# A planner's clock that counts changes of the array's shape, and a ten-point plan of pace for the side work, in a two-block transformer kernel

## The reference

```
x = first_block(x, ...)     # per layer: mixer, layer norm, FFN of 4096, layer norm, gated embedding
x = second_block(x, c, ctx, ...)
# second_block:
for i in range(2):
    mod, mod_c = silu(c) @ w_mod[i] + b_mod[i], silu(c_ctx) @ w_mod[i] + b_mod[i]
    h  = rms_norm(x)  * (1 + sc1)  + sh1
    hc = rms_norm(xc) * (1 + sc1c) + sh1c
    y, yc = token_mixers(h, hc, ...)   # linear attention, neighbourhood and window attention;
                                       # x's three read keys, values and end states of the context
    x = x + g1 * y;  x = x + g2 * swiglu(...)
    if i == 0:
        xc = xc + g1c * yc;  xc = xc + g2c * swiglu(...)
return rms_norm(x, final_norm)
```

## Time and profile before

| | |
|---|---|
| median of 3 runs | 1847.15 us (1845.49 to 1847.87) |
| the profiled execution | 1849.54 us, its span 1848.2 us |
| mean granted TensorE clock | 0.989 |
| TensorE, VectorE, ScalarE busy | 97%, 69%, 54% |
| moved from memory | 331.36 MB, 180 GB/s over the span |

### The profile page before, as it was taken

How to read it: one execution, slowest core, us unless ns; L and a number is a source line. 1 busy time by engine, 2 the same in 40 slices (tenths; PEclk the granted TensorE clock), 3 DMA queues, 4 the chain that set the end, 5 groups by cost and what they waited for, 6 DMA issues and landing times. The chain is left out here.

```text
span 1848.2 us, 35695 instructions
## 1 busy us (share of the span) xinstructions
PE 1783.7 (97%) x14792; PEld 1662.9 (90%) x14792; DVE 1275.3 (69%) x2350; ACT 990.8 (54%) x1741; POOL 76.8 (4%) x81
## 2 busy tenths in 40 slices
PE   7999999999999999999899999999999999989997
PEld 6778899978989999999889987899999998679997
DVE  5566556658779855876676777766677777876665
ACT  4555545456556644654655655554455565644443
POOL 0000100020000200000100001000000000100000
PEclk9999999999999999999999999999999999999999
DMA  9797866686434565455455453445656543236663
GB/s 375 277 346 247 319 189 184 191 287 199 126 115 151 152 185 183 136 161 187 132 173 160 143 166 103 149 160 185 189 177 199 165 149 107 87 116 184 184 185 122
DMA packets 93857, 334.73 MB, mean 181 GB/s; under 512 B 10992, under 2 KB 12976, under 8 KB 93568
## 3 DMA queue, kind: packets, MB, share of 16 engines
q1 hardware_dynamic: 92016, 327.33, 55.4%
q0 software_dynamic: 1680, 5.11, 0.9%
HBM read 331.36 MB, written 1.05 MB: 180 GB/s over the span
## 5 line engine op out<-in xcount | busy, mean ns | idle before, releaser
L565 DVE TENSOR_TENSOR low<-ring,high 128x1024 fp32r<-128x1024 f32 x410 | 501.3, 1224 | 218.6 <-ACT high L557 209.6
L590 PE MATMUL bank<-XHx,high 128*128 128x256 f32 x2096 | 608.2, 290 | 20.9 <-DVE low L565 8.7
L591 PE MATMUL bank<-XLx,high 128*128 128x256 f32 x2096 | 592.0, 282 | 0.0
L592 PE MATMUL bank<-XHx,low 128*128 128x256 f32 x2096 | 590.9, 282 | 0.0
L557 ACT CAST high<-ring 128x1024 fp32r<-128x1024 f32 x410 | 428.4, 1045 | 272.4 <-PE bank L592 225.8
L590 PEld LDWEIGHTS bank<-XHx,high 128*128 128x128 f32 x2096 | 397.7, 190 | 39.3 <-issue 9.1
L591 PEld LDWEIGHTS bank<-XLx,high 128*128 128x128 f32 x2096 | 398.1, 190 | 1.6 <-issue 0.2
L592 PEld LDWEIGHTS bank<-XHx,low 128*128 128x128 f32 x2096 | 398.1, 190 | 0.0
L590 PE MATMUL bank<-XHc,high_side 128*128 128x256 f32 x608 | 180.9, 298 | 9.6 <-DVE low_side L565 7.4
L591 PE MATMUL bank<-XLc,high_side 128*128 128x256 f32 x608 | 172.0, 283 | 0.0
L592 PE MATMUL bank<-XHc,low_side 128*128 128x256 f32 x608 | 171.8, 283 | 0.0
(11 more groups left out here) (448 smaller groups left out, 3054.3 us busy)
## 6 DMA issues: line engine op xcount, KB each, us to landing
ring<-in_stream SPq DMA_DIRECT2D x410, 512.0 KB, 3.7
ring_side<-in_stream SPq DMA_DIRECT2D x110, 512.0 KB, 3.7
ring_mod<-in_stream SPq DMA_DIRECT2D x96, 512.0 KB, 7.8
x_nb<-in_rpb POOLq DMA_DIRECT2D x6, 256.0 KB, 3.5
x_late_NB<-in_rpb POOLq DMA_DIRECT2D x6, 256.0 KB, 3.2
Xx<-in_x SPq DMA_DIRECT2D x2, 512.0 KB, 5.5
Xc<-in_ctx SPq DMA_DIRECT2D x1, 1024.0 KB, 6.6
out<-y SPq DMA_DIRECT2D x8, 128.0 KB, 2.0
```

The costliest lines, as they stand in the source:

```text
L565: nc.vector.tensor_tensor(st.low[:, j % st.n_ring, :], st.ring[:, j % st.n_ring, :], st.high[:, j % st.n_split, :].bitcast(F32), ALU.subtr ...
L590: nc.tensor.matmul(out, wh, xh, start=(i == 0), stop=False)
L591: nc.tensor.matmul(out, wh, xl, start=False, stop=False)
L592: m = nc.tensor.matmul(out, wl, xh, start=False, stop=(c == ks[-1]))
```

## The change

Three things change. TensorE's lane remembers how many rows and columns of the array the last matmul used; `shape(rows, cols)`, called ahead of each matmul or group of them, adds 0.2 us to the clock when they differ. The costs of matmuls are new: `T_us` divides by 2370 and has no added 0.006, a product's passes cost `n / 2180` each, the 64-row and 64-column matmuls of the recurrence 0.03 us each, and the modulations lose 0.45 us per four tiles. And both plans of pace have new points. No instruction, buffer, semaphore or size is added, removed or changed; only the order in the engines' queues and the numbers that hang on it can differ.

```diff
+    def shape(self, rows, cols):
+        if (rows, cols) != self.rows_cols:
+            self.clock += SHAPE_US
+            self.rows_cols = rows, cols
...
 def T_us(n, passes=1):
-    return max(n * passes / 2270.0, 0.06) + 0.006
+    return max(n * passes / 2370.0, 0.06)
+
+
+def pass_us(n):
+    return n / 2180.0
+
+
+SHAPE_US, QUARTER_US = 0.2, 0.03
...
+            T.shape(P, P)
             nc.tensor.matmul(out, wh, xh, start=(i == 0), stop=False)
...
-                m.then_inc(*T.tick(k.s_products, 3 * T_us(n), key, *used))
+                m.then_inc(*T.tick(k.s_products, 3 * pass_us(n), key, *used))
...
+                T.shape(P, 32)
                 T.wait_ge(k.s_raw_mod[tile % RING_MOD], k.marks["mod raw", tile])
...
-                if c % MOD_BATCH == 0:
-                    T.spend(0.45)
...
+            T.shape(HD, P)
             for step in range(len(parts[0])):
...
                 us = T_us(SEQ - q0, 4 // len(one))
+                T.shape(P, P // len(one))
...
-                        m.then_inc(*T.tick(k.s_mixers, T_us(CH, 2), (tag(i), "inner scores", hh)))
+                        m.then_inc(*T.tick(k.s_mixers, QUARTER_US, (tag(i), "inner scores", hh)))
...
-MOD_PLAN = [(0, 0), (120, 16), (200, 48), (385, 72), (440, MOD_TILES)]
-SIDE_PLAN = [(480, 0), (840, 35), (1300, 94), (1530, 110)]
+MOD_PLAN = [(0, 0), (120, 16), (180, 56), (395, 72), (450, MOD_TILES)]
+SIDE_PLAN = [(480, 0), (600, 11), (725, 23), (845, 40), (960, 50), (990, 64), (1200, 80), (1295, 99), (1410, 100), (1535, 110)]
```

More of the change, by code:

```diff
@@ L633, in rows_product @@
             if c == DC - 1:
-                m.then_inc(*T.tick(k.s_products, 3 * T_us(n), keys[i], *mine))
+                m.then_inc(*T.tick(k.s_products, 3 * pass_us(n), keys[i], *mine))
             elif mine:
-                m.then_inc(*T.tick(st.s_used, 3 * T_us(n), *mine))
+                m.then_inc(*T.tick(st.s_used, 3 * pass_us(n), *mine))
             else:
-                T.spend(3 * T_us(n))
+                T.spend(3 * pass_us(n))
             yield None
@@ L1596, in tensor_hgrn @@
     k.bank_of[tag, "inner"] = b0
+    T.shape(P, CH)
     for i in range(2 * NQ):
@@ L1620, in tensor_hgrn @@
         r = slice(j * CH, (j + 1) * CH)
+        T.shape(CH, P)
         for h in range(2):
@@ L1833, in tensor_gla @@
                 k.bank_of[tag(i), "inner", hh] = yield from w.banks.take(T, (tag(i), "masked", hh))
+            T.shape(HD, CH)
             for c in range(CHUNKS):
@@ L1856, in tensor_gla @@
             s = slice(j * CH, (j + 1) * CH)
+            T.shape(CH, P)
             nc.tensor.matmul(k.bank[banks[j]][:, tile * P:(tile + 1) * P], keT[s, tile, :],
                              V_[s, tile, pair * P:(pair + 1) * P], start=True, stop=True).then_inc(
-                *T.tick(k.s_states, T_us(P, 4), (tag(i), "step", n)))
+                *T.tick(k.s_states, T_us(P, 3), (tag(i), "step", n)))
         yield None
@@ L1869, in tensor_gla @@
         halves = [slice(hh * HD, (hh + 1) * HD) for hh in range(2)]
+        T.shape(P, HD)
         for tile in range(NQ):
@@ L1884, in tensor_gla @@
                 state = S[:, n - 1, :]
+            T.shape(HD, HD)
             for hh, r in enumerate(halves):
@@ L1887, in tensor_gla @@
                                      one["q"][r, c * CH:(c + 1) * CH], start=False, stop=True, skip_group_check=True)
-                T.spend(T_us(CH, 2))
+                T.spend(QUARTER_US)
         m.then_inc(*T.tick(k.s_values, 0.0, (tag(i), "sums")))
```

7 lines of the change are left out of this document (4 added, 3 removed).

## The result

The changed kernel takes 1851.2 us (median of 9 executions, 1847.67 to 1856.45), the kernel before 1845.56 beside it (9 executions, 1843.93 to 1848.56). The ratio is 1.0022 with a 95% interval of 1.0012 to 1.0032, so it is slower, by a little. The forecast was 1839 us.

A forecast was written before the change was run, and what follows sets the result against it. TensorE, busy 97% of the span, was taken as the bound. Terms -7.6 + 1.5 - 2 = -8.1 from the profiled 1849.5 gave 1841.4; the median lies 2.4 lower, so 1839 us, range 1827 to 1854.

The forecast's parts named there:

- 845 to 1000: Stretch with two long TensorE waits for side tiles and low clock behind them: -7.6 us, bounds 0 and -15.2.
- Shape changes: Changes of array shape between matmuls, whole kernel: no step orders by them, 0 us, bounds -2 and +2.
- What the time can change by: Whole kernel: TensorE's work is constant; only idle time, lower-clock time and shape-change cost can move.
- What moves the order is mostly the table: Planner: the clock's two corrections nearly cancel, net about 2 to 10 us, so the plan's new points set the order.
- The side work follows the plan closely: Splits of side tiles: the plan sets them, on a clock some 20 to 30 us below the profile's time.
- Modulations: Modulation tiles, judged at 180 us: already ahead of the old plan, so cost 0, bounds -1 to +1.
- The small waits: Some 10 us of TensorE waits besides the two long ones: as many new as removed, 0, bounds -6 and +6.
- The surge: Plan's 14 side tiles in 30 us from 960: only 6 or 7 possible, so +1.5 us, bounds 0 and +10.
- The end of the side work: Last side product some 4 us earlier, leaving more x work to cover last-layer attention: -2 us, bounds -4 and +4.
- Slower by the surge: Rival: TensorE stands at late-landing side tiles, +7 to +10 us, 1854 to 1857 with long waits kept; chance 0.19.
- More changes of shape: Rival: side products between x's small recurrence matmuls after 990, +4 us, 1851; chance 0.07 with other losing reorderings.
- Nothing measurable: Rival: the two long waits only move with x's norms; 1843.5 to 1850.8, about 1847 us; chance 0.18.

The follow-up runs named there:

- before_again: The kernel before, unchanged, run and profiled a second time: ratio 1.0006 [0.9998, 1.0015] to the kernel before.
- clock_late: Changed kernel with both old plans, and old matmul costs and free shape changes once all 110 side tiles are used: 1.0089 [1.0070, 1.0107] to the kernel before.
- after_again: The changed kernel, unchanged, run and profiled again: ratio 1.0013 [1.0001, 1.0026] to the kernel before, median 1850.18 us.

## Why the prediction was wrong

The time lay inside the range of 1827 to 1854, but it moved the other way than was forecast. Two terms of the sum failed: *845 to 1000*, put at -7.6 us and worth -2.6, which new waits elsewhere took back, and *Shape changes*, put at 0, where the last stretch grew by 3.9.

*What the time can change by* was right. All traces have 14,792 matmuls, and the spans differ by idle time and by matmuls at the lower clock.

*"What moves the order is mostly the table"* was wrong, and it is the main error. I had summed the clock's corrections to a net of 2 to 10 us and taken that as small. The clock alone gave 1.0080 and 1.0092, the table alone 1.0006. 4 us of the plan's place are enough for 0.5 to 0.8%, so a net of 2 to 10 us is not small.

*"The side work follows the plan closely"* was wrong before 845: 31 splits and not 37. The distance of the planner's clock from the profile's time, 20 to 30 us, was also worked out too small: with 3 to 5.5 tiles missing or unused at 0.1 to 0.13 tiles per us the same rows give some 30 to 55 us. Between 725 and 845 there are 10 splits in both kernels. My guess from the stage times is that the contexts' attention, which must end first, holds the work there; no run tested it.

*Modulations, 0:* held. The old modulation plan gave 1.0009 [0.9999, 1.0019] beside 1.0013 [1.0001, 1.0026].

*845 to 1000, -7.6:* failed; it carried the forecast. The wait by VectorE's order fell from 5.4 to 3.4 us, the wait for the DMA stayed (4.4 and 4.5). Together 9.8 became 7.9, 1.9 less. The low clock behind them cost 5.4 us and now costs 0.30 of 5.6 and 0.50 of 6.0, 4.7. That makes 2.6 us and not 7.6. *The small waits, 0:* failed too. The other waits for side tiles grew, from 2.5 to 5.9 us and in the second traces from 3.6 to 5.1; the largest of them is one of 2.95 us at 1212, in both traces of the changed kernel, where before has 1.0 and 1.3. The wait of 1.9 us for `c_gla_end` is new as well. Up to V idle time didn't change.

*The surge, +1.5:* 5 splits in its 30 us for 3, where 6 or 7 were forecast, and no wait for `low_side` between 980 and 1120 in either trace, so the cost that was forecast isn't there. Without the point the ratio is 1.0043.

*The end of the side work, -2:* the sign was wrong in effect. c's last product did come 4 us earlier in the profiled execution, at 1556.6 for 1560.8, but before_again, with the old order, has it at 1556.4: that was no effect of the order. What came in that place is +3.9 us behind it.

*Shape changes, "no step orders by them", 0 with bounds -2 and +2:* this is where the loss is. The price moves TensorE's lane against VectorE's in the planner, and so it can shift the splits among the softmax steps. Taking it away behind the side work is worth 5.5 to 7.5 us of the last stretch over the two traces of either kernel, and 0.38% between the ratios. It is shown that in this order the price causes the block. By which tie in the planner it does so was not followed, and clock_late shows that the block can come without it.

*Rivals.* "Slower by the surge" is excluded: between 980 and 1120 TensorE waits for no side tile, and the kernel without the surge is no faster. "More changes of shape" names the time, 1851, but not the cause: the order of TensorE has not more changes than before (277 by the same count that gave 285). The Trainium skill (TensorEngine Tiling (Array Packing), Key Properties) says that a change of mode drains TensorE; the trace agrees with a cost of about 0.09 us, but what the price did to VectorE's queue outweighs it. "Nothing measurable" is nearest for the middle.

**What stays open.** Six neighbours of the changed kernel under the new clock (points 4 us earlier, 4 us later, no surge, the price at 0.1 and at 0, the old plans) are all slower than it, by 0.2 to 1.0% and each with waits of its own. A seventh, with only the old modulation plan, is not slower (1.0009). That fits points chosen for this very clock among many orders. Why the old clock is less touchy (1.0006 and 1.0021 for its two neighbours) isn't settled by two runs.

## What to carry to other kernels

Where a planner orders engines by an estimated clock and a table of times is set against that clock, the two are one thing: change one and the whole order is drawn anew, here for -0.3 to +1.2%, even where the correction is small, so time the neighbours too before you believe in a mechanism. Compare stretches that hold the same matmuls, not windows of equal time: it put a loss of 0.2% into one place, though executions of one order differ by as much. And a more faithful price is not a better one where the planner doesn't act on what it prices: free behind the side work and 0.2 us ahead of it gave 0.9973 and 0.9975, the best of all.

## What the runs showed of the hardware

The same order with the same wait can be followed by the lower clock or not. Around 1209 the changed kernel waits 2.95 us for a side tile in both its traces. In the first the clock stays at 1.00:

```profile
1209.40:1213.40 4.00, 1.17 (x9) 1.17 (x10) 4.00 (x9) 3.23 (x7) 0.00 (x0) 1.00 0.44 131
1213.40:1217.00 3.60, 3.60 (x33) 3.60 (x32) 3.60 (x8) 2.37 (x5) 0.00 (x0) 1.00 0.02 5
```

In after_again it falls to 0.50, 1.2 GHz:

```profile
1209.60:1213.70 4.10, 1.52 (x12) 1.52 (x13) 4.10 (x10) 3.40 (x7) 0.00 (x0) 1.00 0.44 132
1213.70:1217.10 3.40, 3.40 (x18) 3.40 (x17) 3.40 (x8) 1.37 (x4) 0.00 (x0) 0.50 0.00 0
```

Half of such a stretch is lost, 1.7 us. The kernel before has two of them (at 188.8 and 1199.1) which before_again, the same program, doesn't have; at 1.7 us each that is most of the 4.1 us between their spans. Two executions of one order can so differ by more than this whole change is worth, and an order that saves a wait of some 2 us may save the stretch behind it too.

The Trainium skill (TensorE: Matmul & The Clock Gate, Part 1) says that the number of slow matmuls at the start of a kernel varies from run to run. The two traces show the same of a place in the middle of one.
